# Second attention: sums over keys in high and low parts, moved into the next round

## The reference, cut to what matters

```python
def mixer_b(x, w_in, w_o, k, v):
    q, gate = jnp.split(x @ w_in, [WIDTH_B], axis=-1)
    ...
        z = jnp.einsum('bqngd,bsnd->bngqs', qg, k).astype(jnp.float32) * (HEAD_DIM ** -0.5)
        strict = key_pos[None, :] < t[:, None]
        log_om = jnp.where(strict, -jax.nn.softplus(z), 0.0)
        suffix = lax.cumsum(log_om, axis=log_om.ndim - 1, reverse=True) - log_om
        a = jnp.where(strict, jnp.exp(jax.nn.log_sigmoid(z) + suffix), 0.0)
        o = jnp.einsum('bngqs,bsnd->bqngd', a.astype(v.dtype), v)
    ...
    return (o * jax.nn.silu(gate)) @ w_o
```

## Time and profile before

| | us |
|---|---|
| runs, median of 3 | 2741.19 (2740.61 to 2742.47) |
| the profiled execution, its own time | 2739.0 |
| its span, first to last instruction | 2737.3 |
| PE busy | 2712.9 (99%) |
| DVE busy | 1550.2 (57%) |
| ACT busy | 1295.7 (47%) |
| POOL busy | 57.6 (2%) |

### The profile page before, as it was taken

How to read it: one execution, slowest core, us unless ns; L and a number is a source line. 1 busy time by engine, 2 the same in 40 slices (tenths; PEclk the granted TensorE clock), 3 DMA queues, 4 the chain that set the end, 5 groups by cost and what they waited for, 6 DMA issues and landing times.

```text
span 2737.3 us, 34409 instructions
## 1 busy us (share of the span) xinstructions
PE 2712.9 (99%) x12254; PEld 2227.3 (81%) x12254; DVE 1550.2 (57%) x1904; ACT 1295.7 (47%) x1697; POOL 57.6 (2%) x66
## 2 busy tenths in 40 slices
PE   9999999999999999999999999999999999999999
PEld 7888888888888788888888888877888888777877
DVE  6555555555735466555555555757555576555566
ACT  6443444344544445443444344545544554554453
POOL 0000000000000000000000000030000000120000
PEclk9999999999999999999999999999999999999999
DMA  9876677676745476765676666754455576445654
GB/s 313 249 207 195 209 217 207 193 215 182 257 140 177 147 230 215 222 210 192 208 216 209 194 213 187 258 171 154 151 192 182 171 223 208 154 139 196 187 176 138
DMA packets 414584, 540.63 MB, mean 198 GB/s; under 512 B 40080, under 2 KB 262544, under 8 KB 413680
## 3 DMA queue, kind: packets, MB, share of 16 engines
q1 hardware_dynamic: 412800, 530.46, 62.1%
q0 software_dynamic: 1504, 8.34, 0.8%
q10 hardware_dynamic: 144, 0.04, 0.0%
HBM read 520.34 MB, written 18.35 MB: 197 GB/s over the span
## 4 chain that ended last, share of the span: by engine, by line
PE 93%; DVE 2%; DMA 1%; ACT 1%; POOL 1%; SPq 1%; issue 1%; ACTq 0%; POOLq 0%; DVEq 0%
PE bank L1325 29%; PE bank L1327 29%; PE bank L1326 29%; DVE wlo L1666 1%; PE bank L1284 1%; DMA raw<-in_ffn_w_in_dram 1%; SPq L1206 1%; POOL rope_b L884 1%; ACT whi L1412 1%; PE bank L1031 0%; DMA hidden_squares<-hidq 0%; PE bank L832 0%; PE bank L816 0%; PE bank L1048 0%; PE bank L1057 0%
## 5 line engine op out<-in xcount | busy, mean ns | idle before, releaser
L1666 DVE TENSOR_TENSOR wlo<-raw,whi 128x1024 fp32r<-128x1024 f32 (+2 forms) x975 | 1150.0, 1186 | 1112.5 <-ACT whi L1412 1107.4
L1412 ACT CAST whi<-raw 128x1024 fp32r<-128x1024 f32 (+2 forms) x975 | 986.1, 1016 | 1304.5 <-PE bank L1327 1297.8
L1325 PE MATMUL bank<-whi,p_hi 128*128 128x512 f32 x2016 | 794.6, 394 | 4.5 <-DVE wlo L1666 3.2
L1327 PE MATMUL bank<-whi,p_lo 128*128 128x512 f32 x2016 | 785.0, 389 | 0.0
L1326 PE MATMUL bank<-wlo,p_hi 128*128 128x512 f32 x2016 | 784.7, 389 | 0.0
L1325 PE MATMUL bank<-whi,q_hi 128*128 128x512 f32 x1696 | 665.2, 392 | 2.8 <-DVE wlo L1666 2.8
L1327 PE MATMUL bank<-whi,q_lo 128*128 128x512 f32 x1696 | 660.4, 389 | 0.0
L1326 PE MATMUL bank<-wlo,q_hi 128*128 128x512 f32 x1696 | 660.0, 389 | 0.0
L1325 PEld LDWEIGHTS bank<-whi,p_hi 128*128 128x128 f32 x2016 | 378.4, 188 | 91.2 <-issue 13.2
L1326 PEld LDWEIGHTS bank<-wlo,p_hi 128*128 128x128 f32 x2016 | 378.6, 188 | 80.1 <-issue 3.1
L1327 PEld LDWEIGHTS bank<-whi,p_lo 128*128 128x128 f32 x2016 | 378.4, 188 | 79.7
(11 more groups left out here) (274 smaller groups left out, 1009.5 us busy)
## 6 DMA issues: line engine op xcount, KB each, us to landing
raw<-in_ffn_w_in_dram SPq DMA_DIRECT2D x704, 256.0 KB, 3.0
raw<-in_ffn_w_out_dram SPq DMA_DIRECT2D x320, 256.0 KB, 3.1
raw<-in_w_in_a_dram SPq DMA_DIRECT2D x192, 256.0 KB, 3.1
raw<-in_w_in_mix_dram SPq DMA_DIRECT2D x128, 256.0 KB, 3.2
raw<-in_w_ple_gate_dram SPq DMA_DIRECT2D x128, 256.0 KB, 3.9
raw<-in_w_in_b_dram SPq DMA_DIRECT2D x128, 256.0 KB, 3.1
raw<-in_w_out_mix_dram SPq DMA_DIRECT2D x64, 256.0 KB, 3.5
raw<-in_w_o_a_dram SPq DMA_DIRECT2D x64, 256.0 KB, 3.4
```

Of the source, the lines that this page charges most:

```text
L1325: pe.matmul(o, xht, wh, start=(kt == t_first), stop=False)
L1327: ins = pe.matmul(o, xlt, wh, start=False, stop=(kt == t_last))
L1412: act.copy(whi[:, c % SPLIT, 0:n, 0:w], raw[:, c, 0:n, 0:w]).then_inc(hi_done, 1)
L1666: dve.tensor_tensor(wlo[:, c % SPLIT, 0:n, 0:w], raw[:, c, 0:n, 0:w], whi[:, c % SPLIT, 0:n, 0:w].bitcast(F32), ALU.subtract).then_inc(lo_ ...
```

## The change

The softplus of each unit is kept as two fp32r parts: ACT copies it to a high part (step c = 7 of its round), DVE subtracts to a low part (step c = 0 of the next round), and PE makes each of the four products as two fp32r products (step c = 1 of the next round), with fp32r copies of the constant matrices made once. The steps behind move: DVE's additions to c = 1, Exp to c = 2, the weighted values to c = 6, their copies to c = 6. The query transposes move from c = 1 to 2, all scores to c = 3, ACT's softplus steps to 3 and 4, DVE's to 4 and 5. The weights x get a second set of places for odd groups. The order of the banks changes: a round now takes fb of the group before, qb, zb, and then ob of the group before. POOL's order is unchanged. The diff, cut:

```diff
-                      [("b_proj", [P, TT, 3072], F32), ("unit_q", [P, 4, NB], F32)])
+                      [("b_proj", [P, TT, 3072], F32), ("unit_q", [P, 4, NB], F32)],
+                      [("b_proj_pad", [P, TT, 3072], F32), ("unit_qr", [P, 4, NB], F32R)])
...
+                      [("pad_b", [P, 2048], F32), ("unit_b", [P, 3, NB], F32), ("signs_b", [P, 2 * P], F32R)],
...
+                      [("unit_er", [P, 5, NB], F32R)],
...
-            for g in range(KVH):
-                for name, m in (("qb0", 0), ("qb1", 1), ("ob0", 2), ("ob1", 3), ("zb0", 0), ("zb1", 1), ("zb2", 2),
-                                ("fb0", 3), ("fb1", 0), ("fb2", 1)):
-                    if name[0] != "o":
-                        plan(f"{name}_{g}", m)
-                    elif g:
-                        plan(f"{name}_{g - 1}", m)
-            for name, m in (("ob0", 2), ("ob1", 3)):
-                plan(f"{name}_{KVH - 1}", m)
+            for g in range(KVH + 1):
+                for name, m, back in (("fb0", 3, 1), ("fb1", 0, 1), ("fb2", 1, 1), ("qb0", 0, 0), ("qb1", 1, 0),
+                                      ("zb0", 0, 0), ("zb1", 1, 0), ("zb2", 2, 0), ("ob0", 2, 1), ("ob1", 3, 1)):
+                    if 0 <= g - back < KVH and (back or g < KVH):
+                        plan(f"{name}_{g - back}", m)
...
         def unit(i):
             places = [aq["unit_q"][:, n, :] for n in range(4)] + [ae["unit_e"][:, n, :] for n in range(5)]
-            return places[3 * i:3 * i + 3]
+            return places[3 * i:3 * i + 2]
+        def weight(i, g):
+            places = [aq["unit_q"][:, n, :] for n in range(4)] + [ae["unit_e"][:, n, :] for n in range(5)]
+            return ab["unit_b"][:, i, :] if g % 2 else places[3 * i + 2]
+        def summed_parts(i):
+            places = [aq["unit_qr"][:, n, :] for n in range(4)] + [ae["unit_er"][:, n, :] for n in range(5)]
+            whole = 1 if i == 1 else 0
+            return places[3 * i + 1 - whole], places[3 * i + whole], unit(i)[whole]
         def last_group(stage, k):
...
-            if before is not None and c == 2:
-                pe.wait_ge(sem("weights_masked"), 2 * before + 2)
-                pe.wait_ge(sem("stick_exp"), 3 * before + 3)
...
...
-            if c == 1:
+            if before is not None and c == 1:
+                pe.wait_ge(sem("signs_done"), 1)
+                pe.wait_ge(sem("summed_split"), 3 * before + 3)
+                wait_freed(pe, f"zb1_{before}")
+                ntri, nones = (ab["signs_b"][:, n * P:(n + 1) * P] for n in range(2))
+                for i in range(3):
+                    b = use(f"fb{i}_{before}")
+                    terms = [(ntri, part) for part in summed_parts(i)[:2]]
+                    if i == 1:
+                        terms += [(nones, part) for part in summed_parts(2)[:2]]
+                    for n, (signs, part) in enumerate(terms):
+                        ins = pe.matmul(b[:, :], signs, part, start=(n == 0), stop=(n == len(terms) - 1))
+                    filled(ins, f"fb{i}_{before}")
+            if g is not None and c == 2:
...
-            if c in (2, 3):
-                for i in ((0, 1), (2,))[c - 2]:
+            if g is not None and c == 3:
+                for i in range(3):
...
-            if c == 7:
-                pe.wait_ge(sem("softplus_masked"), 2 * g + 2)
-                wait_freed(pe, f"zb1_{g}")
-                summed = [unit(0)[0], unit(1)[1], unit(2)[0]]
-                for i in range(3):
-                    b = use(f"fb{i}_{g}")
-                    ins = pe.matmul(b[:, :], const("ntri"), summed[i], start=True, stop=(i != 1))
-                    if i == 1:
-                        ins = pe.matmul(b[:, :], const("nones"), summed[2], start=False, stop=True)
-                    filled(ins, f"fb{i}_{g}")
+            if before is not None and c == 6:
+                pe.wait_ge(sem("weights_masked"), 2 * before + 2)
+                pe.wait_ge(sem("stick_exp"), 3 * before + 3)
+                for t in range(TT):
+                    b = use(f"ob{t}_{before}")
+                    for i in range(4):
+                        for st in range(t + 1):
+                            ins = pe.matmul(b[:, i * P:(i + 1) * P], weight(t + st, before)[:, i * P:(i + 1) * P],
+                                            proj[:, st, BV + before * P:BV + (before + 1) * P], start=(st == 0), stop=(st == t))
+                    filled(ins, f"ob{t}_{before}")
         def attention_b_act(act, stage, k, c):
...
-            if before is not None and c == 0:
+            if (stage, k, c) == ("b_q", 0, 1):
+                for t in range(TT):
+                    release(act.copy(proj[:, t, BK:BK + NB], take(act, f"kb{t}")[:, :]), f"kb{t}")
+                act.wait_ge(acc_free, by_name["gate0"].a0 + by_name["gate0"].n + FREE0)
+                act.copy(ab["signs_b"][:, :], con[:, CONST["ntri"] * P:(CONST["nones"] + 1) * P]).then_inc(sem("signs_done"), 1)
+            if g is not None and c == 2:
+                for t in range(TT):
+                    release(act.activation(proj[:, t, g * NB:(g + 1) * NB], take(act, f"qb{t}_{g}")[:, :], ACT.Copy,
+                                           scale=float(HD) ** -0.5), f"qb{t}_{g}")
+            if c == 1 and (g is not None or before is not None):
+                act.preload_act_table_set("natural_log_exp_and_others")
+            if before is not None and c == 2:
...
-                    x = unit(i)[2]
+                    x = weight(i, before)
...
...
-            if c == 1:
...
-                act.preload_act_table_set("natural_log_exp_and_others")
-            if c in (2, 3):
-                for i in ((0, 1), (2,))[c - 2]:
+            if c in (3, 4):
+                for i in ((0, 1), (2,))[c - 3]:
...
+            if c == 7:
+                for i in (1, 0, 2):
+                    if i == 1:
+                        wait_freed(act, f"zb1_{g}")
+                    else:
+                        act.wait_ge(sem("softplus_masked"), 2 * g + i // 2 + 1)
+                    hi_, _, whole = summed_parts(i)
+                    act.copy(hi_, whole).then_inc(sem("summed_hi"), 1)
         def attention_b_dve(dve, link, stage, k, c):
...
-            if before is not None and c == 2:
...
-            if g is None:
-                return
-            if c in (3, 4):
-                for i in ((0, 1), (2,))[c - 3]:
-                    lo_, sp_, x = unit(i)
+            if before is not None and c == 0:
+                for n, i in enumerate((1, 0, 2)):
+                    dve.wait_ge(sem("summed_hi"), 3 * before + n + 1)
+                    hi_, lo_, whole = summed_parts(i)
+                    dve.tensor_tensor(lo_, whole, hi_.bitcast(F32), ALU.subtract).then_inc(sem("summed_split"), 1)
+            if before is not None and c == 1:
+                for i in range(3):
+                    x = weight(i, before)
+                    release(dve.tensor_tensor(x, x, take(dve, f"fb{i}_{before}")[:, :], ALU.add), f"fb{i}_{before}")
+            if g is not None and c in (4, 5):
+                for i in ((0, 1), (2,))[c - 4]:
+                    lo_, sp_ = unit(i)
...
-                    release(dve.tensor_tensor(x, b[:, :], sp_, ALU.subtract), f"zb{i}_{g}")
-            if c == 7:
...
+                    release(dve.tensor_tensor(weight(i, g), b[:, :], sp_, ALU.subtract), f"zb{i}_{g}")
+            if before is not None and c == 6:
+                for t in range(TT):
+                    release(dve.tensor_copy(tm[:, t, before * NB:(before + 1) * NB], take(dve, f"ob{t}_{before}")[:, :]), f"ob{t}_{before}")
         def mixer_b_pool(pool):
...
-                    lo_, sp_, _ = unit(i)
+                    lo_, sp_ = unit(i)
...
-                    x = unit(i)[2]
+                    x = weight(i, g)
```

More of the change, by code:

```diff
@@ L1023, in attention_b_pe @@
                     filled(ins, f"kb{t}")
-            if before is not None and c == 2:
+            if before is not None and c == 1:
[12 more added lines that the diff above has]
+            if g is not None and c == 2:
+                pe.wait_ge(acc_free, by_name["b_q"].a0 + g + 1 + FREE0)
+                for t in range(TT):
+                    b = use(f"qb{t}_{g}")
+                    for i in range(4):
+                        ins = pe.transpose(b[:, i * P:(i + 1) * P], proj[:, t, g * NB + i * P:g * NB + (i + 1) * P], ident)
+                    filled(ins, f"qb{t}_{g}")
+            if g is not None and c == 3:
+                for i in range(3):
+                    t, st = PAIRS[i]
+                    wait_freed(pe, f"kb{st}")
+                    wait_freed(pe, f"qb{t}_{g}")
+                    filled(pe.matmul(use(f"zb{i}_{g}")[:, :], proj[:, st, BK + g * P:BK + (g + 1) * P],
+                                     proj[:, t, g * NB:(g + 1) * NB], start=True, stop=True), f"zb{i}_{g}")
+            if before is not None and c == 6:
                 pe.wait_ge(sem("weights_masked"), 2 * before + 2)
```

(43 more changed lines are left out.)

## The result

The median of four executions is 2761.4 us (2758.6 to 2762.7) against 2740.9 (2740.6 to 2742.5) before: a ratio of 1.0072, 95% interval 1.0055 to 1.0090. That is 20.5 us slower, where 11.7 had been forecast, and outside the range given. The profiled execution took 2760.5, its span 2758.8, against 2739.0 and 2737.3.

The account below looks back on a forecast made before the run. PE, busy throughout the attention's rounds, was taken as the bound. Terms -6.5 - 0.5 + 11.8 + 6.9 = +11.7 took the profiled 2739.0 to 2750.7; with 2.2 for the median, 2752.9 us, range 2747 to 2758.

Parts of the forecast that it names:

- What bounds the kernel: In the attention's rounds PE is busy throughout, so time taken from its list or spent waiting there changes the total.
- The saving, 6.5 + 0.5: On PE, fp32r products replacing fp32 ones over four groups save 6.5 us; the last round's wait on POOL's mask saves 0.5.
- the row: The trace's fp32 product price, 3.8 pitches (0.86 us), used instead of the skill's four passes: saving 6.5, not 7.3.
- The wait for the sums, 2.6, 2.6, 2.6 and 4.05: PE stands ahead of the sums for DVE's low parts, in four rounds: together 11.8 us, bounds 6.9 to 13.0.
- The wait for the bank, 2.3: PE's weighted values wait until DVE has read unit 2's scores from the shared bank: three rounds, together 6.9 us.
- rival (c), the clock: PE's clock falls in a wait: 2755.6 with one chunk slowed behind the last, 2763.8 behind all four sums' waits; 8%.
- The prediction's own sign of being wrong: The forecast is wrong if PE's waits in these rounds sum to under 12 us, or the granted clock is under 1.00.
- The range: 2747 to 2758 us for the whole kernel, letting in one fall of the clock.

Follow-up runs that it names:

- the kernel with both edits: Changed kernel with DVE's low parts made in step c = 7 of their own round and ob0, ob1 on other banks: 2732.1 us, ratio 0.997.
- the edits: Changed kernel with low parts early (2745.1 us), with ob0, ob1 on other banks (2751.5), and with both except low parts late in the last round (2739.9).

## Why the prediction was wrong

- **What bounds the kernel**: right. Every wait of PE showed up in full, and with none left the saving did.
- **The saving, 6.5 + 0.5**: right. 3.44 became 1.81 a group, and the kernel with both edits gained 7.5 at equal clock. The arithmetic alone is worth 6.6 between the same two matmuls, where the trace's 3.44 - 1.81 gives 6.5. The Trainium skill's four passes for fp32 (FP8 and Floating Point Precision, TensorE Precision Notes), taken at the fp32r product's pace of 0.227, would give 7.3; the measured 6.6 speaks for the row.
- **The wait for the sums, 2.6, 2.6, 2.6 and 4.05**: right, 2.50 three times and 4.19. The three copies went at 0.52 each as taken from the nearest form.
- **The wait for the bank, 2.3**: right in mechanism, 2.51 in size. The bank was free when forecast: L1131 ended at 2400.55, the first score started at 2387.54, 13.01 apart against 12.98. But the matmul started 0.26 behind it, where 0.06 had been read off POOL's row.
- **The failed step is rival (c), the clock.** The sum put the clock at nothing. I had a fall behind one or perhaps all waits of the sums as a rival, at 8%, and argued from the earlier trace rows that waits of 2.2 and 2.4 had left the clock at 1.00 in the profiled execution. That was one execution, and the 2.4 should not have counted: it lies ahead of PE's first matmul, at 2.35, where no dense work stood before it. The 2.2 is one of a pair of such waits, near 2047 and 2506, and it was luck that neither had a fall in that trace: over the nine traces the clock fell behind 6 of these 18. In the traces after, the clock fell behind 12 of 15 unfilled waits of 2.5 to 4.2: 5 of 7 in the changed kernel, 3 of 3, 3 of 4 and 1 of 1 in the edits. By the windows ten of the twelve falls cost 1.7 and two 3.4 (in the one shown above 0.6 of it inside the wait); I had priced one at 2.7, too much for most. The term that stood at nothing measured 8.4, and the waits 19.2 for 18.7: 2752.9 + 8.4 + 0.5 = 2761.8, against 2761.4. The prediction's own sign of being wrong was met too: the granted clock of the profile after is 0.997. The Trainium skill's warning against idle gaps between bursts of matmuls (TensorE: Matmul & The Clock Gate, Why this matters for your kernels), which I cited and gave little weight, is borne out, and here by shorter gaps than those that the page names: the clock fell behind nine of twelve waits with 2.3 to 2.4 us of idle time.
- **The range** was drawn from the waits' bounds with one fall let in. A case against which the rows have no more than two waits should have had a chance nearer one half, and the range should have reached 2764.

## What to carry to other kernels

On an in-order engine with a fixed schedule, a step's operands must be finished by the step's place in the other engines' lists, not in the same numbered slot: here what DVE made in its step c = 0 was done 2.4 us after PE had come to its step c = 1 (2377.59 against 2375.19), and what it made one step earlier was in time. When the banks' order is rewritten, name for each bank who frees it and when. And price a wait of TensorE of some 2.5 us at one and a half times its length where the array runs densely around it (2.5, and 1.7 three times in four here; 4.2 and 1.7 or 2.8 for the longer one). If such a wait can't be removed, products that are overwritten can stand in it: here they took 8.4 us off. And don't take a full clock in one profiled execution for a rule: the kernel before had it in 6 of 18.

## What the runs showed of the hardware

A wait of TensorE of 2.5 us in a stream of back-to-back matmuls was followed in 9 of 12 cases by a time at 1.2 GHz that cost 1.7 us; one of 4.2 us in all three traces, at a cost of 1.7 once and 3.4 twice, of which 0.6 or 0.7 lay inside the wait. Useless products in the first 0.9 us of each wait kept the clock up in the trace of that run, and filling the waits whole gave 8 us of 20 back. The kernel before, too, has executions with a mean clock of 0.999, and they are its slower ones: of eighteen, twelve have 0.999 and a median of 2741.9, six have 1.000 and 2739.1.
